# A two-block transformer kernel: the second half of the first block's values is projected as four feature tiles between the attention heads

## The reference, cut to what matters

```
h = rmsnorm(x, norm1_w)
aq, ak, av, bq, bk, bv, br, ba, cq, ck, cv = split(h @ w_in)
y_a = dilated_attention(aq, ak, av)       # 6 heads of 64
y_b = gla(bq, bk, bv, br, ba)             # 4 heads, chunks of 16
y_c = moba_attention(cq, ck, cv)          # 6 heads of 64
x = x + concat(y_a, y_b, y_c) @ w_out
```

## Time and profile before

| what | us |
|---|---|
| median of three runs | 2450.49 |
| profiled execution | 2452.98 |
| its span | 2451.2 |
| TensorE busy | 2336.9 (95%) |
| VectorE busy | 1410.3 (58%) |
| ScalarE busy | 901.4 (37%) |
| GpSimd busy | 513.0 (21%) |

### The profile page before, as it was taken

One profiled execution on the slowest core, in us unless ns is written; L12 is line 12 of the kernel. 1 busy time (PEld: TensorE's weight loads), 2 busy tenths in 40 slices (PEclk: granted clock), 3 DMA queues, 4 the chain that ended last, 5 costly groups with the idle time before them and its releaser, 6 DMA issues.

```text
span 2451.2 us, 29863 instructions
## 1 busy us (share of the span) xinstructions
PE 2336.9 (95%) x11514; PEld 1834.6 (75%) x11514; DVE 1410.3 (58%) x2253; ACT 901.4 (37%) x1536; POOL 513.0 (21%) x385
## 2 busy tenths in 40 slices
PE   7989799999999998889999999999999989999998
PEld 5655578888877875658888888888676667788886
DVE  4475648888666456664575565544636774434335
ACT  4244533322343224773422222122421783423232
POOL 3332223222212200001322121111121002322221
PEclk9999899999999999999999999999999999999999
DMA  4211016555411231011243343421122112322321
GB/s 164 90 52 53 26 52 227 192 182 197 157 65 55 92 96 36 18 35 35 82 138 121 116 134 121 131 97 57 54 91 85 34 35 69 104 86 95 103 86 52
DMA packets 76249, 227.69 MB, mean 93 GB/s; under 512 B 9152, under 2 KB 12609, under 8 KB 76109
## 3 DMA queue, kind: packets, MB, share of 16 engines
q1 hardware_dynamic: 70928, 216.69, 26.4%
q0 software_dynamic: 1856, 6.07, 0.7%
q10 hardware_dynamic: 3324, 3.02, 0.4%
HBM read 220.99 MB, written 4.76 MB: 92 GB/s over the span
## 4 chain that ended last, share of the span: by engine, by line
PE 51%; DVE 2%; ACT 1%; POOL 1%; issue 1%; DVEq 0%; ACTq 0%; POOLq 0%
PE psum L685 23%; PE psum L949 18%; PE psum L1256 2%; PE psum L654 2%; PE psum L1287 2%; PE psum L1271 1%; PE psum L1145 1%; PE psum L603 0%; PE psum L1210 0%; PE psum L1104 0%; PE psum L1223 0%; PE psum L620 0%; DVE mla_stat L2115 0%; DVE mla_probT L2126 0%; PE psum L1171 0%
## 5 line engine op out<-in xcount | busy, mean ns | idle before, releaser
L685 PE MATMUL psum<-mix_split,weight_split 128*128 128x512 f32 (+1 forms) x3456 | 714.0, 368 | 2.4 <-POOL weight_split L2746 1.1
L685 PEld LDWEIGHTS psum<-mix_split,weight_split 128*128 128x128 f32 x3456 | 590.9, 188 | 122.3 <-POOL weight_split L2746 1.5
L949 PE MATMUL psum<-hidden,weight_split 128*128 128x512 f32 (+1 forms) x3072 | 633.2, 367 | 0.0
L949 PEld LDWEIGHTS psum<-hidden,weight_split 128*128 128x128 f32 x3072 | 524.5, 188 | 105.3
L2196 ACT CAST weight_split<-weight_ring 128x1024 fp32r<-128x1024 f32 x269 | 277.1, 1042 | 301.7 <-PE psum L949 236.6
L2746 POOL TENSOR_TENSOR weight_split<-weight_ring,weight_split 128x1024 fp32r<-128x1024 f32 x89 | 234.0, 2629 | 604.2 <-ACT weight_split L2196 603.6
L1724 DVE TENSOR_TENSOR hidden<-hidden_tmp,hidden 128x512 fp32r<-128x512 f32 (+1 forms) x128 | 157.1, 1248 | 315.9 <-POOL hidden_tmp L2867 315.9
L1366 DVE TENSOR_TENSOR weight_split<-weight_ring,weight_split 128x1024 fp32r<-128x1024 f32 x180 | 231.7, 1289 | 40.0 <-ACT weight_split L2196 40.0
L2867 POOL TENSOR_TENSOR hidden_tmp<-hidden_tmp 128x512 f32<-128x512 f32 (+1 forms) x128 | 125.0, 988 | 614.7 <-ACT hidden L2449 614.6
L2445 ACT ACTIVATE hidden_tmp<-psum 128x512 f32<-128x512 f32 (+1 forms) x128 | 69.0, 539 | 495.0 <-PE psum L685 494.9
L1741 DVE SCALAR_TENSOR_TENSOR residual<-psum,modulation,residual 128x512 f32<-128x512 f32 x192 | 120.1, 657 | 161.3 <-PE psum L949 160.9
(11 more groups left out here) (317 smaller groups left out, 2497.2 us busy)
## 6 DMA issues: line engine op xcount, KB each, us to landing
weight_ring<-in_w_mlp SPq DMA_DIRECT2D x128, 512.0 KB, 3.8
weight_ring<-in_w_ff SPq DMA_DIRECT2D x64, 512.0 KB, 4.6
mod_ring<-in_w_mod SPq DMA_DIRECT2D x48, 512.0 KB, 3.7
late_ring<-in_w_mod SPq DMA_DIRECT2D x96, 256.0 KB, 3.7
weight_ring<-in_w_in SPq DMA_DIRECT2D x45, 512.0 KB, 3.6
weight_ring<-in_w_out SPq DMA_DIRECT2D x24, 512.0 KB, 3.5
weight_ring<-in_tables SPq DMA_DIRECT2D x13, 512.0 KB, 3.5
weight_ring<-in_w_v SPq DMA_DIRECT2D x8, 512.0 KB, 3.9
```

The costliest lines, as they stand in the source:

```text
L685: m = pe.matmul(psum[:, b + r, 0:hi - lo], w[:, part_w, :], x[:, part_x, k, lo:hi], start=k == 0 and part_w + part_x == 0, stop=k == KT - ...
L949: mm = pe.matmul(psum[:, b + r, 0:hi - lo], w[:, part_w, :], G[:, part_x, f % (2 * GROUP), lo:hi], start=jj == 0 and part_w + part_x == 0, ...
```

## The change

Half 0 of the values stays as it is. Half 1 is no longer made by `project_values`. Its 512 columns become four more tiles, 17 to 20, which are projected feature-major like all others, between the heads. Each is kept in `mix_7`, a buffer not used at that time, turned by four transposes of TensorE (`turn_values`, after turns 16, 24, 32 and 35), and copied by ScalarE to its place in `V` one turn later. The next of them may be kept when the last one is turned.

`FILL` gives the tiles of each head: heads 1, 3, 5 and 7 have two, the others one, head 11 none. Where there are two, a half is projected ahead of each of the four turns, and the keeps stand in turns 4u+1 and 4u+3. The order of `IN1` becomes 16, 6, 7, 0, 3, 1, 4, 2, 5, 10, 13, 17, 11, 14, 18, 12, 15, 19, 20, 8, 9, and with it the engine of each keep.

With half 1 eight half ticks go, so each linear-attention step comes one head later than before; its list of pair steps starts with shift 1 in head 0 instead of shift 5. `ROOTS` stays at 102, `GATES` goes from (105, 113) to (101, 105), `SPLIT_MIX` from 113..119 to 105..111.

```diff
-        IN1 = [16, 6, 7, 0, 3, 1, 4, 2, 5, 10, 13, 11, 14, 12, 15, 8, 9]
+        FILL = [[4], [2, 5], [10], [13, 17], [11], [14, 18], [12], [15, 19], [20], [8], [9], []]
         BEFORE = 6
+        IN1 = [16, 6, 7, 0, 3, 1] + [i for tiles in FILL for i in tiles]
+        V_TILES = [17, 18, 19, 20]
+        V_TURN = {16: 17, 24: 18, 32: 19, 35: 20}
...
+        def filled(n):
+
+            u, r = divmod(n, 4)
+            tiles = FILL[u]
+            return [tiles[r // 2]] if len(tiles) == 2 and r % 2 else [] if len(tiles) == 2 else tiles if r == 2 else []
+
+        def staged(n):
+
+            u, r = divmod(n, 4)
+            return FILL[u][r // 2:r // 2 + 1] if r % 2 == 0 else []
...
+            if i in V_TILES:
+                return mix_7[:, :]
...
+            if i in V_TILES[1:]:
+                return [("in1_pe", ("turned", i - 1))]
...
-        GATE, VT, PAIR, KTOK, U_AT, CARRY, GATES, ROOTS = 4, 14, 18, 50, 53, 81, (105, 113), 102
+        GATE, VT, PAIR, KTOK, U_AT, CARRY, GATES, ROOTS = 4, 14, 18, 50, 53, 81, (101, 105), 102
...
+            def turn_values(i):
+
+                b = take(1, "turn")
+                bank_of["in1", "turned", i] = b
+                wait_bank(b)
+                pe.wait_ge(*when(*in1_keep(i)))
+                for t in range(4):
+                    m = pe.transpose(psum[:, b, t * P:(t + 1) * P], in1_home(i)[:, t * P:(t + 1) * P], C["ident"][:, :])
+                m.then_inc(*did("in1_pe", ("turned", i)))
+                freed[b] = [("in1_act", ("v_tile", i))]
...
-                for half, banks in enumerate(((0, 1, 6, 7), (3, 0, 1, 6))):
-                    for _ in project_values(half, banks):
-                        half_tick()
+                for _ in project_values(0, (0, 1, 6, 7)):
+                    half_tick()
...
-                    halves = iter(()) if filler(u) is None else project(filler(u))
+                    halves = itertools.chain.from_iterable(project(i) for i in FILL[u])
                     next(halves, None)
                     if u and u % 2 == 0:
                         values(u // 2 - 1)
                     for n in range(4 * u, 4 * u + 4):
-                        if n == 4 * u + 2:
+                        if n % 4 == 2 or n % 4 and len(FILL[u]) == 2:
+                            next(halves, None)
+                        if n % 4 == 3:
                             for _ in halves:
                                 pass
                         turned(n)
                         if n % 2 == 0 and n + 4 < len(ATT):
                             logits(n + 4)
+                        if n in V_TURN:
+                            turn_values(V_TURN[n])
                         half_tick()
                         half_tick()
...
-                        if n == 4 * u + 2 and filler(u) is not None:
-                            keep(filler(u))
+                        for i in filled(n):
+                            keep(i)
```

More of the change, by code:

```diff
@@ L2 @@
+import itertools
 import math
@@ L390, in in1_keep, with v_of @@
             return ("in1_vec" if IN1.index(i) % 2 else "in1_act"), ("keep", i)
+        def filled(n):
[5 more added lines that the diff above has]
+            return FILL[u][r // 2:r // 2 + 1] if r % 2 == 0 else []
+        def v_of(x, i):
+            c = 512 + P * V_TILES.index(i)
+            return V[:, :, c:c + P], x.rearrange("p (t c) -> p t c", c=P)
         def in1_home(i):
+            if i in V_TILES:
+                return mix_7[:, :]
             for p, pair in enumerate(PAIRS):
@@ L410, in in1_home_free @@
                     return [("att_pe", ("logits", 8 * (p - 1) - 1))]
+            if i in V_TILES[1:]:
+                return [("in1_pe", ("turned", i - 1))]
             return []
[L413 to L422 removed]
+        GATE, VT, PAIR, KTOK, U_AT, CARRY, GATES, ROOTS = 4, 14, 18, 50, 53, 81, (101, 105), 102
+        SPLIT_MIX = {105: 0, 106: 1, 107: 2, 108: 5, 109: 6, 110: 3, 111: 4}
         OUT_ORDER, OUT_CUTS = [0, 1, 2, 5, 6, 3, 4, 7], (2, 4, 6, 7)
@@ L846, in values @@
                 if p == 0:
-                    for half in range(2):
-                        for t in range(4):
-                            pe.wait_ge(*when("in1_vec" if t % 2 else "in1_act", ("v", half, t)))
+                    for t in range(4):
+                        pe.wait_ge(*when("in1_vec" if t % 2 else "in1_act", ("v", 0, t)))
+                if p > 1:
+                    pe.wait_ge(*when("in1_act", ("v_tile", V_TILES[p - 2])))
                 pe.wait_ge(*when("att_act", ("probT", 8 * p + 6)))
@@ L1645, in mixers @@
                 half_tick()
-                for half in range(2):
+                for half in range(1):
                     for s in range(4):
@@ L1683, in mixers @@
                                 split_mix_1(SPLIT_MIX[at[0] - 1])
-                        if n == 4 * u and filler(u) is not None:
-                            stage("w_in1", filler(u))
+                        for i in staged(n):
+                            stage("w_in1", i)
                 mix(NH // 2 - 1)
@@ L2383, in mixers @@
                 for u in range(NH):
-                    if filler(u) is not None:
-                        stage("w_in1", filler(u))
                     for n in range(4 * u, 4 * u + 4):
+                        for i in staged(n):
+                            stage("w_in1", i)
                         if n + 3 < len(ATT):
@@ L2389, in mixers @@
                         prob_t(n)
+                        if n - 1 in V_TURN:
+                            i = V_TURN[n - 1]
+                            ac.wait_ge(*when("in1_pe", ("turned", i)))
+                            ac.copy(*v_of(bank(bank_of["in1", "turned", i]), i)).then_inc(*did("in1_act", ("v_tile", i)))
                         if n + 4 < len(ATT):
@@ L2829, in mixers @@
                 half_tick()
[L2830 to L2834, removed]
+                for s in range(4):
+                    half_tick()
+                    stage("w_v1", (0, s))
+                    half_tick()
                 for i in IN1[3:BEFORE]:
@@ L2840, in mixers @@
                     for n in range(8):
-                        if n == 2 and filler(u) is not None:
-                            stage("w_in1", filler(u))
+                        if n % 4 == 2:
+                            for i in staged(4 * u + n // 2 - 1):
+                                stage("w_in1", i)
                         half_tick()
@@ L3008, in sync_program @@
                 sy.dma_start(X[:, 2 * i:2 * i + 2, 0:S], dr["x_t"][:, 2 * i:2 * i + 2, :]).then_inc(x_sem[i], 16)
-            fill(load_at["w_in1", filler(1)])
+            fill(load_at["w_in1", FILL[1][0]])
             sy.wait_ge(rows_sem, 16)
@@ L3014, in sync_program @@
                 if u > 1:
-                    fill(load_at["w_in1", IN1[min(BEFORE + u, len(IN1) - 1)]] + AHEAD)
+                    fill(load_at["w_in1", (FILL[u] or IN1)[-1]] + AHEAD)
                 if u == 3:
@@ L3091, in lay_out @@
     ba = np.concatenate([w[:, BA:BA + B_RANK], np.zeros((D, P - B_RANK), np.float32)], 1)
-    d["w_in1"] = np.stack([tiles(w, slice(s, s + P)) for s in starts] + [slots_of(ba)])
-    wv = np.concatenate([w[:, BV:BV + 256], w[:, AV:AV + 384], w[:, CV:CV + 384]], 1)
-    d["w_v1"] = np.ascontiguousarray(wv.reshape(4, 2, P, 2, 512).transpose(3, 0, 2, 1, 4).reshape(2, 4, P, 1024))
+    d["w_in1"] = np.stack([tiles(w, slice(s, s + P)) for s in starts] + [slots_of(ba)] + [tiles(w, slice(s, s + P)) for s in (AV + 2 * P, CV, CV + P, CV + 2 * P)])
+    wv = np.concatenate([w[:, BV:BV + 256], w[:, AV:AV + 256]], 1)
+    d["w_v1"] = np.ascontiguousarray(wv.reshape(4, 2, P, 512).transpose(0, 2, 1, 3).reshape(1, 4, P, 1024))
     d["w_out1"] = np.stack([tiles(a["w_out"][0], c) for c in cols(KT)])
```

## The result

The changed kernel takes 2461.8 us (median of four runs, 2460.39 to 2468.39) against 2450.65 for the kernel before: ratio 1.0049, 95% interval 1.0038 to 1.0061, 11.2 us slower. The forecast was 2459.8. The profiled execution took 2460.87 us with a span of 2459.1, 7.9 us more than that of before.

What follows compares the result with a forecast made beforehand. TensorE was taken to bound the kernel, with 17.9 us idle in the heads. Terms 0 - 1.85 + 1.4 + 13.0 - 1.8 + 0 - 1.5 = +9.3 us on the 2450.49 us median gave 2459.8 us, range 2444 to 2470.

Steps and rivals of the forecast that it cites:

- The move itself: Projection matmuls moved from ahead of the heads into heads 1, 3, 5, 7: 23.0 us go, 23.0 come, 0.
- The eight waits: Heads 1, 3, 5, 7: TensorE waits for PSUM bank 6 with one turn of cover, +13.0 us (4 to 23).
- The rival of the short waits: VectorE and ScalarE run ahead, so bank 6 waits total only 5 to 7 us: 2453 us, chance 0.23.
- Waits that change: Existing waits: bank 6 -1.8 us, pairs in head 1 -2.2, VectorE's fuller head 0 +2.2; sum -1.8 us.
- The normalisation: Linear attention's normalisation on ScalarE moves from turn 37 to 41: taken as 0, bounds -1.6 to +4.9 us.
- The clock: TensorE's granted clock in the heads: part comes back in head 7, head 0 worsens; -1.5 us (-6.5 to +9).
- The last rival: Clock falls to 0.88 in heads 1, 3, 5, 7, losing 9 us: +20 us, 2470 us, chance 0.09.
- The rival of the filled idle time: Dense halves between turns keep the clock up, pair waits go, bank waits total 4 us: 2443 us, chance 0.18.

Runs made afterwards that it cites:

- e1_keep_first: Changed kernel, but in heads with two tiles the copy out of bank 6 stands ahead of that turn's softmax work: 2451.03 us, 1.0004 of the kernel before.
- e2_turn_later: Changed kernel, but value tiles are turned after turns 18, 26, 34 and 38 instead of 16, 24, 32 and 35: 2458.19 us, 1.0042 of the kernel before.
- e0_after: Changed kernel unaltered, timed again as a base: 2462.25 us, 1.0052 of the kernel before.
- e6_second_bank: Changed kernel with bank 7 as a second PSUM bank for the projections in heads 4 to 7: 2462.31 us, 1.0039 of the kernel before.
- e3_both: Changed kernel with both edits, copy first in two-tile heads and value tiles turned later: 2443.07 us, 0.9970 of the kernel before.
- e8_both_again: e3_both unaltered, run again: 2443.52 us, 0.9966 of the kernel before.
- e10_all_first: e3_both with the copy ahead of the softmax work in heads with one tile as well: 2435.31 us, 0.9944 of the kernel before.
- e11_all_first_again: e10_all_first unaltered, run again: 2437.03 us, 0.9943 of the kernel before.

## Why the prediction was right

**The total, and what is luck in it.** The sign and the mechanism, waits for bank 6, are right, and the size is near: 2461.8 us for 2459.8. But the sum was made for the mixers, +9.3 us, and there the two profiles of the changed kernel show +13.5 and +15.5. Head 10 starts 14.0 us later, not 9. Of the 4.2 us that the first profile adds, 3.2 are TensorE's busy time (+1.3 for a forecast -1.95) and 1.0 is idle time. The program behind the mixers, for which the sum had nothing, took 5.6 and 6.4 us less than before. That it brought the total back near the forecast is luck.

**The move itself, 0.** Nothing speaks against it. TensorE's busy time in the mixers went from 216.0 to 217.3 us, for a predicted change of -0.45 without the clock and -1.95 with it. The terms around it were too small: the four groups of transposes took 2.3 us and not 1.4, and shifts 1 to 4 in head 0 some 6.5 and not 5.35, the last four of these matmuls at a granted clock of 0.52. The first transpose of head 0 starts at 91.90, where 92 to 94 had been named.

**The eight waits, +13.0.** 13.35 measured. One by one, forecast and measured: 1.3 and 1.37, 2.25 and 2.13, 2.1 and 1.89, 1.8 and 1.82, 1.0 and 0.88, 0.9 and 1.78, 2.4 and 2.26, 1.2 and 1.22. The outlier is turn 23. The copy was no later than forecast: TensorE had the bank 2.77 us after the transpose had ended, for 2.85. But the state updates ran side by side, four in 1.05 us, where I had taken 1.95 us off as cover. e1_keep_first takes 12.4 us of the eight away, and the time falls by 11.2 us. The rival of the short waits, 5 to 7 us in all, is refuted by the same rows.

**Waits that change, -1.8.** The old bank waits fell by 4.4 rather than 1.8 us: that of head 8 is gone too, since TensorE now waits at `turn_values(20)`, and is late enough when it comes to the bank. Head 1's pair waits are gone as said. Head 0 waits 3.6 us instead of 2.2, of which 2.6 are one wait for GpSimd's product, and head 2 waits 3.3; pairs as a whole 6.9 against 7.1.

**What was missed.** The price of `turn_values` was taken as its 1.4 us of transposes. That it takes a turn of the three transpose banks just behind the values product was not seen: +4.07 us, shown by e2_turn_later. It is partly cancelled by the larger fall of the old bank waits (2.6 more than forecast), so the total hides two errors. The two belong together in part: the 1.89 us at `turn_values(20)` stand in place of the 2.04 us behind head 8, so what is new is 2.2 us. Idle time rose by 12.2 us against 11.2 in the sum.

**The normalisation, 0.** Right for the total: from the start of head 10 to the first output matmul are 19.9 us against 20.4, and head 10 and 11 take 42.8 against 43.3. Only the place of the waiting differs. Before, TensorE waited 1.6 us at the values product, 2.9 at the logits of head 11 and 3.9 at the first output matmul, 8.4 in all; now it is 7.5 at the last of them:

```profile
303.59 2.90 PE L904 MATMUL psum<-mix_split,weight_split 128*128 128x512 f32 x6 [7.47 <-DVE mix_split L1614]
307.92 1.67 PE L904 MATMUL psum<-mix_split,weight_split 128*128 128x512 f32 x6 [1.43 <-POOL mix_split L2848]
...
312.11 1.66 PE L904 MATMUL psum<-mix_split,weight_split 128*128 128x512 f32 x6 [0.78 <-POOL mix_split L2848]
...
323.83 2.87 PE L904 MATMUL psum<-mix_split,weight_split 128*128 128x512 f32 x6 [2.68 <-POOL mix_split L2848]
```

**The clock, -1.5.** Not borne out. The granted clock in the mixers was 0.93 against 0.94 before. Halves of a projection with a part at the low level (4 to 5.5 us instead of 3) were five against four, in heads 1, 2, 7, 8 and 9. The last rival, 0.88 in all four heads with two tiles and 9 us lost, does not come in that size: they ran at 0.90, 1.00, 1.00 and 0.92. But its mechanism is there. In the second profile of the same kernel, e0_after, they ran at 0.94, 0.85, 1.00 and 1.00, and the prediction had named a clock under 0.9 in head 3 as the sign of this rival. Heads 3 to 7 show it best, first in the two profiles of the changed kernel and then in e1_keep_first:

```profile
151.09:246.71 95.62, 83.82 (x420) 53.25 (x419) 47.28 (x136) 40.45 (x93) 27.63 (x25) 0.98 0.19 61
150.24:247.42 97.18, 85.39 (x419) 54.38 (x419) 47.23 (x136) 40.66 (x93) 27.62 (x25) 0.96 0.19 60
147.05:231.72 84.67, 82.12 (x420) 52.10 (x419) 46.48 (x134) 39.96 (x90) 27.62 (x25) 1.00 0.22 69
```

The matmuls are the same, but TensorE needs 83.8 and 85.4 us for them with the waits for bank 6, and 82.1 without. e2_turn_later and e6_second_bank, which keep all or half of these waits, have 0.96 as well; e3_both, e8_both_again and the two with all copies first, which don't, have 1.00 and 82.0 to 82.1 us. So the waits cost some 1.7 to 3.3 us more than their own length. The Trainium skill's rule in "TensorE: Matmul & The Clock Gate", section "A second HAM failure mode: psum-queue depth-cycling", by which brief waits for banks pull the clock down, agrees with this in its direction; in which heads the clock falls changes from run to run, and head 5 stayed at 1.00 in both profiles, with waits of 0.88 and 1.78.

**The rival of the filled idle time** failed as argued: the heads that got most of the tiles had no idle time. Heads 1, 3, 5 and 7 took 22.7, 19.5, 21.2 and 21.2 us, where 18 to 21 had been named. What it asked for, keeps within 0.5 us of need, is what e3_both makes, and there the time is the 2443 that it named, though the pair waits stayed and turning later had a part in it.

## What to carry to other kernels

Work that moves into a stretch bound by the same engine gains little by itself (here a few us, once the copies stood first); count the idle time of the very places where it goes, then the buffers that it has to pass. A copy that frees a single bank belongs ahead of any work in its engine's program that waits for something later; here this was worth 11 us, and a second bank, which had to be taken from somebody, nothing that shows. Brief waits of the busiest engine can cost more than their length, as its clock may fall with them: here by 1.7 to 3.3 us in heads 3 to 7. A new user of a rotating pool moves everybody behind it by one place: look whose slow release now comes next.

## What the runs showed of the hardware

The program behind the mixers is the same in all of these kernels, yet it took 2138.2 us in the profile of the kernel before and 2132.6 in that of the changed one (from the remaining output tiles to the end of the span), and 2129.0 in that of e10_all_first. Part of the difference lies around the end of the first block. The stretch there, before and after (columns as in the first table):

```profile
710.00:790.00 80.00, 74.38 (x386) 59.14 (x384) 55.02 (x88) 31.52 (x53) 13.30 (x11) 0.89 0.12 42
```

```profile
722.00:798.00 76.00, 70.36 (x388) 56.59 (x387) 55.60 (x89) 31.53 (x53) 13.30 (x11) 0.96 0.13 44
```

With nearly the same matmuls, TensorE's granted clock is 0.89 in the one and 0.96 in the other, and the offset between the kernels shrinks over them from 12.5 to 8.1 us, by 4.4. So a change of 13 us in one place was one of 8 in the profiled span and 11 in the medians. What decides which such stretch gets the low level these runs do not show. The 80 us that begin 397 us after the remaining output tiles had 0.96 in the first profile of the changed kernel and 0.91 in its second. Against pure chance speaks that they had 0.91 in both e3_both and e8_both_again, 0.96 in both e10_all_first and e11_all_first_again, and that the last two agree in their medians, 2435.3 and 2437.0. But the time at which the program gets there is not all of it: e10_all_first and e11_all_first_again are one kernel, reach the remaining output tiles within 0.1 us of each other (302.16 and 302.21), and took 2129.0 and 2132.5 us from there. So differences of some 3 us between single profiles are not to be read as an effect of a change.
